# One base address and eight weight slabs: h starts at 480 modulo 512, and the gates of four output tiles are multiplied in the last SSD iteration

## The reference

```python
h = rmsnorm(x)
z, xBC, dt, q, f, i, g, gate_a, gate_b = split(h @ w_in)
y   = chunked_scan(conv(xBC), dt, state)          # Mamba-2 SSD, 8 groups
y   = grouped_rmsnorm((y + D * xs) * silu(z))     # 8 groups of 512 columns
y_a = y @ w_br_a                                  # 4096 -> 2048
y_b = hgrn2(q, f, i, g, state) @ w_br_b           # 2048 -> 2048
m   = sigmoid(gate_a) * y_a + sigmoid(gate_b) * y_b
x   = x + rmsnorm(m @ w_out)
x   = x + rmsnorm(relu(rmsnorm(x) @ w_up)**2 @ w_down)
x   = x + sigmoid(rmsnorm(x) @ w_ple_gate) * (p @ w_ple_proj)
```

## Time and profile before

| | us |
|---|---|
| median of 3 runs | 2816.43 |
| time of the profiled execution | 2817.92 |
| its span, first to last instruction | 2816.0 |
| TensorE busy | 2742.1 (97%) |
| VectorE busy | 1789.6 (64%) |
| ScalarE busy | 1425.6 (51%) |
| HBM read and written | 483.4 MB, 172 GB/s over the span |
| chain that ended last, by engine | PE 88%, DVE 7%, ACT 2%, issue 1%, DMA 1% |

### The profile page before, as it was taken

How to read it: one execution, slowest core, us unless ns; L and a number is a source line. 1 busy time by engine, 2 the same in 40 slices (tenths; PEclk the granted TensorE clock), 3 DMA queues, 4 the chain that set the end, 5 groups by cost and what they waited for, 6 DMA issues and landing times.

```text
span 2816.0 us, 59589 instructions
## 1 busy us (share of the span) xinstructions
PE 2742.1 (97%) x22075; PEld 2662.8 (95%) x22075; DVE 1789.6 (64%) x3208; ACT 1425.6 (51%) x2280; POOL 183.1 (7%) x297
## 2 busy tenths in 40 slices
PE   6999999999999999999979999989999999999999
PEld 5999999999999999999969999989999999999989
DVE  6878788744478887888854444566553345554475
ACT  5666666543356556556633333454443344443363
POOL 0111111100011111111110000000000000000000
PEclk9999999999999999999979999999999999999999
DMA  4544454455556665656535555535555545554534
GB/s 159 181 159 158 160 172 161 156 168 174 177 199 196 197 204 200 210 191 209 189 135 171 173 172 181 190 128 169 165 165 164 165 163 164 164 168 161 171 129 159
DMA packets 135286, 484.17 MB, mean 172 GB/s; under 512 B 17248, under 2 KB 19696, under 8 KB 134080
## 3 DMA queue, kind: packets, MB, share of 16 engines
q1 hardware_dynamic: 114560, 410.88, 43.8%
q0 software_dynamic: 20672, 72.55, 8.0%
HBM read 449.58 MB, written 33.78 MB: 172 GB/s over the span
## 4 chain that ended last, share of the span: by engine, by line
PE 88%; DVE 7%; ACT 2%; issue 1%; DMA 1%; POOL 0%; DVEq 0%; ACTq 0%; POOLq 0%
PE acc L1583 27%; PE acc L1585 26%; PE acc L1584 26%; DVE w_lo L967 1%; PE bank L1800 1%; PE bank L1846 1%; ACT w_hi L496 1%; PE bank L1749 1%; DVE ccv L1240 1%; PE bank L1830 1%; PE bank L1684 1%; PE bank L1766 0%; DVE x L1427 0%; DVE yf L1297 0%; DVE ht L1226 0%
## 5 line engine op out<-in xcount | busy, mean ns | idle before, releaser
L967 DVE TENSOR_TENSOR w_lo<-raw,w_hi 128x1024 fp32r<-128x1024 f32 x772 | 940.2, 1223 | 617.9 <-ACT w_hi L496 611.1
L1583 PE MATMUL acc<-h_hi,w_hi 128*128 128x288 f32 x3904 | 1169.6, 300 | 14.0 <-DVE h_lo L1003 11.5
L1584 PE MATMUL acc<-h_lo,w_hi 128*128 128x288 f32 x3904 | 1154.6, 296 | 0.0
L1585 PE MATMUL acc<-h_hi,w_lo 128*128 128x288 f32 x3904 | 1151.2, 295 | 0.0
L496 ACT ACTIVATE w_hi<-raw 128x1024 fp32r<-128x1024 f32 x772 | 811.3, 1055 | 463.8 <-PE acc L1585 408.0
L1583 PEld LDWEIGHTS acc<-h_hi,w_hi 128*128 128x128 f32 x3904 | 734.6, 188 | 21.7 <-issue 12.3
L1584 PEld LDWEIGHTS acc<-h_lo,w_hi 128*128 128x128 f32 x3904 | 735.9, 189 | 2.9
L1585 PEld LDWEIGHTS acc<-h_hi,w_lo 128*128 128x128 f32 x3904 | 737.7, 189 | 0.0
L1585 PE MATMUL acc<-u_hi,w_lo 128*128 128x288 f32 x1024 | 303.6, 296 | 0.0
L1583 PE MATMUL acc<-u_hi,w_hi 128*128 128x288 f32 x1024 | 302.6, 296 | 0.0
L1584 PE MATMUL acc<-u_lo,w_hi 128*128 128x288 f32 x1024 | 298.5, 292 | 0.0
(11 more groups left out here) (389 smaller groups left out, 3336.1 us busy)
## 6 DMA issues: line engine op xcount, KB each, us to landing
raw<-in_w SPq DMA_DIRECT2D x772, 512.0 KB, 3.3
ht<-in_ht POOLq DMA_DIRECT2D x64, 256.0 KB, 4.1
out_ssm_s<-ht POOLq DMA_DIRECT2D x64, 256.0 KB, 3.8
cbc<-cum_d POOLq DMA_DIRECT2D x8, 1152.0 KB, 6.9
hs<-in_s POOLq DMA_DIRECT2D x16, 512.0 KB, 4.5
out_hg_s<-hsn POOLq DMA_DIRECT2D x16, 512.0 KB, 5.0
x_in<-in_x SPq DMA_DIRECT2D x4, 576.0 KB, 6.0
mixb<-bmb POOLq DMA_DIRECT2D x16, 144.0 KB, 2.0
```

The costliest lines, as they stand in the source:

```text
L967: V.tensor_tensor(w_lo[:, k], raw[:, k], w_hi[:, k].bitcast(F32), ALU.subtract).then_inc(lo_done, 1)
L1583: M.matmul(out, w_hi[:, k, i], hi[:, kt0 + i], start=first and i == 0, stop=False)
L1584: M.matmul(out, w_hi[:, k, i], lo[:, kt0 + i], start=False, stop=False)
L1585: op = M.matmul(out, w_lo[:, k, i], hi[:, kt0 + i], start=False, stop=last and i == SK - 1)
```

## The change

First, `place[0] = aligned(place[0])` before h_hi and before the phase area: every base is rounded up to 480 modulo 512. Before, h_hi lies at byte 65664 and h_lo at 84096 of a partition (both 128 modulo 512); after, at 66016 and 84448 (both 480). The phase area, where o, y and u lie, moves from 111584 to 112096, which is 480 before and after; m stays at 192480 (480). The weights `w_hi` and `w_lo` stay at 32896 and 49280 (both 128). The constants move with h; `p_hi` comes to 480, `p_lo` stays at 224 modulo 512 at another address, and `p_in` takes the place of tok.

Second, the gate slabs of output tiles 0 to 3 (EARLY = 4) come first in the order of slabs: eight gate slabs, then 4 x 4 slabs of y. The eight are multiplied in the tail, into four banks; the y slabs of tiles 0 to 3 follow and use bank[2] and bank[3].

```diff
+EARLY = 4
 STORED = {}
+for _t in range(EARLY):
+    for _s in range(GA_SLABS):
+        STORED[U_GA + (2 * _t + _s if _s < 2 else 2 * EARLY + 4 * _t + _s - 2)] = U_GA + GA_SLABS * _t + _s
...
+    def aligned(at):
+
+        return (at - 480 + 511) // 512 * 512 + 480
...
+    place[0] = aligned(place[0])
     h_hi = sb("h_hi", [P, KT, T], F32R)
...
-    phase = place[0]
+    phase = place[0] = aligned(place[0])
...
+    gate_bank = (ps[0], ps[1], bank[0], bank[1])
...
+            def early_gate(u):
+
+                t = u // 2
+                if u % 2 == 0:
+                    if t < 2:
+                        free(T_GA + t, 0)
+                    elif t == 2:
+                        pe.wait_ge(sg_yf, 4 * GROUPS)
+                    else:
+                        pe.wait_ge(sg_spe, GROUPS)
+                multiply(*slab(U_GA, 2 * GA_SLABS, 0, u), gate_bank[t][:, 0:T], h_hi, h_lo, SK * (u % 2),
+                         u % 2 == 0, u % 2 == 1)
...
                 if not gemm:
+                    if s < 4:
+                        early_gate(s)
+                    if s in (7, 8):
+                        early_gate(s - 3)
+                    if s == 11:
+                        early_gate(6)
+                        early_gate(7)
                     continue
```

More of the change, by code:

```diff
@@ L697, in ssd @@
                 nxt(s)
+                if not gemm and s == 8:
+                    ahead(U_GA, 2 * GA_SLABS, 0, 3)
                 if not first and s == 8:
@@ L700, in ssd @@
                     nc.scalar.activation(yt, bank[5][:, :], ACT.Copy).then_inc(sg_yt, 1)
+                if not gemm and s == 9:
+                    ahead(U_GA, 2 * GA_SLABS, 0, 4)
                 if not first and s == 10:
@@ L703, in ssd @@
                     nc.scalar.activation(ysq, yf[:, :, :], ACT.Square).then_inc(sg_sq, 1)
+                if not gemm and s == 11:
+                    ahead(U_GA, 2 * GA_SLABS, 0, 5)
                 if not first and s == 12:
@@ L792, in branch_a @@
                 nc.scalar.activation(aya[:, :], ps[1][:, 0:T], ACT.Copy).then_inc(evac, 1)
[L793 to L798, removed]
+                merged_hi(t)
+        with act.Fori(EARLY // 2, KT // 2) as i:
+            branch_a(i)
         def out_tiles(i, first):
@@ L1289, in ssd @@
                         update({1: 0, 2: 2, 8: 4, 9: 6}[s])
+                    if not gemm and 1 <= s <= 4:
+                        ahead(U_GA, 2 * GA_SLABS, 0, s - 1)
+                    if not gemm and s in (11, 12):
+                        ahead(U_GA, 2 * GA_SLABS, 0, s - 7)
                     if s == 10:
@@ L1378, in _, with merge, branch_a @@
             if c in (1, 3):
-                ahead(U_GA, 2 * GA_SLABS, 0, c // 2)
-        def branch_a(i, first):
+                ahead(U_GA, 2 * GA_SLABS, 0, 6 + c // 2)
+        def merge(t):
+            dve.wait_ge(evac, t * 2 + (T_GA + 2))
+            dve.wait_ge(ga_in, t * 16 + 16)
+            V.scalar_tensor_tensor(aya[:, :], atg[:, :], 1.0, aya[:, :], ALU.add, ALU.mult).then_inc(ga_t, 1)
+            dve.wait_ge(ga_t, t + 1)
+            V.tensor_tensor(aya[:, :], aya[:, :], amb[:, :], ALU.add).then_inc(ga_m, 1)
+            dve.wait_ge(ga_hi, t + 1)
+            V.scalar_tensor_tensor(tile_at(m_lo, t), one(aya[:, :]), 0.5, tile_at(m_hi, t).bitcast(F32),
+                                   ALU.mult, ALU.subtract).then_inc(ga_lo, 1)
+        for t in range(EARLY):
+            for s in range(4):
+                ahead(U_GA, 2 * GA_SLABS, 0, 2 * EARLY + 4 * t + s)
+            merge(t)
+        def branch_a(i):
             for j in range(2):
-                t = i * 2 + j
-                for s in range(2 if first and j == 0 else 0, GA_SLABS):
+                for s in range(GA_SLABS):
                     ahead(U_GA, 2 * GA_SLABS, i, GA_SLABS * j + s)
[L1386 to L1397, removed]
+                merge(i * 2 + j)
+        with dve.Fori(EARLY // 2, KT // 2) as i:
+            branch_a(i)
         def weight(col, t):
@@ L1784, in ssd @@
                         new_states(2)
[L1785 to L1790, removed]
                     if s == 7:
@@ L1858, in _, with branch_a @@
         ssd(GROUPS, False, False)
-        def branch_a(i, first):
+        for t in range(EARLY):
+            if t < 2:
+                pe.wait_ge(sg_up, NB * GROUPS)
+            else:
+                pe.wait_ge(evac, T_GA + 2 * (t - 2) + 2)
+            for s in range(4):
+                multiply(*slab(U_GA, 2 * GA_SLABS, 0, 2 * EARLY + 4 * t + s), bank[2 + t % 2][:, 0:T], y_hi, y_lo,
+                         SK * s, s == 0, s == 3, (y_los, 0) if t == 0 else None)
+        def branch_a(i):
             for j in range(2):
-                for s in range(2 if first and j == 0 else 0, GA_SLABS):
+                for s in range(GA_SLABS):
                     if s in (0, 2):
@@ L1869, in branch_a @@
                     else:
[L1870 to L1875, removed]
+                        multiply(*at, ps[1][:, 0:T], y_hi, y_lo, SK * (s - 2), s == 2, s == 5)
+        with pe.Fori(EARLY // 2, KT // 2) as i:
+            branch_a(i)
         def out_tiles(i, first):
```

34 lines of the change are left out of this document (23 added, 11 removed).

## The result

| us | before | after |
|---|---|---|
| median | 2816.43 (2815.96 to 2818.28) | 2790.62 (2790.40 to 2791.71, 4 runs) |
| profiled execution, its span | 2817.92, 2816.0 | 2790.41, 2788.5 |
| h, second up stage, 512 first-pass matmuls | 204.4 | 202.7 |
| HGRN2, distance from one head to the next | 32.37 | 32.19 |
| SSD, distance from one group to the next | 81.08 | 80.89 |

The ratio is 0.9908 (95%: 0.9891 to 0.9925), the change is worth 25.8 us by the medians, 0.9%. 2788.0 was predicted with a range of 2781 to 2795. Old lines and new: 1583 to 1585 are now 1621 to 1623, 1749 is 1787, 1766 is 1804, 1758 is 1796, 1800 is 1845, 703 is 716, 967 is 995, 1376 is 1408, 2033 is 2092.

A forecast was written before the change was run, and what follows sets the result against it. TensorE was taken as the bound, busy 2742.1 of 2816.0 us. Terms of -13.2 (base address) and -15.2 (tail) sum to -28.4: 2789.5 profiled from 2817.92, 2788.0 as median, range 2781 to 2795.

The forecast's parts named there:

- Rival 2: The offset does nothing for h, which differs by lying just above the weights; 2801.2 us, chance 0.08.
- Rival 4: Slower than before: h's new offsets meet those of w_hi and w_lo in slow steps only; 2833.5 us, chance 0.04.
- the 0.2 I took off: Deduction in us from the 13.4 gained on h slabs, for places where TensorE arrives sooner only to wait.
- part 1: Base address: h takes u's rate, 3.173 for 3.200 us a slab, on 504 dense slabs; -13.2 us, bounds 0 to -14.5.
- Part 2: Tail: six gate slabs move into it, -19.2 us, less the delay to y; -15.2, bounds -21.5 to -10.7.
- (a): Tail, loads of ht: weight loads running beside them make ht arrive 4.0 us later; bounds 0 and 5.
- (b): Tail, gate slabs 0 to 3 on TensorE: they end at 1432.4, before ht lands, and delay nothing.
- (c): Tail, from ht's landing to the first y_lo: 0 us change, between -2.3 at full clock and +3.5 at half.
- (d): Tail, after the first y_lo: VectorE's list sets the pace, so tile 0 ends 17.1 us later, as before.
- (e): Behind tile 0, y slabs alone for tiles 1 to 3: splits and merge are covered by TensorE's 12.7 us.
- Rival 1: Tail: the loads don't collide and the clock holds, so Part 2 is -21.5; 2781.7 us, chance 0.20.
- rival 3: Tail: gate slabs wait for splits, the first y_lo slips 16 us, only 3.2 of Part 2 left; 2800.0, chance 0.06.

## Why the prediction was right, and where it was not

**The sign and the size of the offset, per matmul: right.** 202.7 in place of 204.4 is 132.2 ns a matmul in place of 133.3, as read from u, and the alternation of 0.78 and 0.81 came as said. Rival 2 (the offset does nothing) is out by the experiment with the offset alone. The Trainium skill, page "TensorE: Matmul & The Clock Gate", section "Back-to-back issue gap", gives N / 2.4 + 2.5 ns as the gap of an isolated matmul, and for streams of a weight load and a matmul about 81 ns at 128 columns and 131 at 512; the prediction left the second half out. The 132.2 and 133.3 ns measured at 288 columns are more than either gives, and neither has a term for addresses; the runs show two rates for one shape, sorted by addresses.

**The reason behind it: half right.** I took the rate as a property of the input's own offset. It is the distance to the weights that counts: with u and m untouched and only the weights moved, they lost what h had gained. Rival 4 had the right pair of tensors and the wrong sign: h lay in the slow relation already. The number came out because u and m had the distance +96 when I read them, and h got the same.

**How much of it reaches the end: wrong, the 0.2 I took off should have been 4 to 5.** Worked out from the two traces, part 1 gave 2.6 in the HGRN2 loop (first head to last, 480.85 to 478.21; 120 slabs, 3.2 by count), 1.2 in SSD iterations 1 to 7 (first ht matmul to the tail's old_states(0), 564.25 to 563.06; 140 slabs, 3.7 by count), 0.6 in gate_a, 1.4 in the first up stage, 1.7 in the second, 0.7 at the end: 8.2, where 13.4 - 0.2 were summed. The largest miss is the SSD loop: 0.19 a group in place of 0.53. From old_states(0), behind a group's first slab, to its sum of squares it is 42.16 us in both traces (1176.87 to 1219.03, and 1170.25 to 1212.41): that half is set by VectorE's and ScalarE's chain to xw, and TensorE's gain on the 11 slabs in it is handed back as a longer wait, 0.75 for 0.50. I had that very wait before me and charged it once, 0.2 in all, when it takes back this gain in each of the groups. A further 0.6 is missing in HGRN2, some 0.5 in the later stages, whose cause I didn't look for.

The 52 slabs of gate_b and of the SSD's first iteration, 1.4 by count, are in none of these terms, as their gain can't be told from noise: the stretch with them, from the last head to the first ht matmul, is 292.5 before and 289.5 after, but 289.5 too with h at its old place. Before's profiled execution had two more stretches at half clock there (3.4 us each), by chance. That is 3 us of the 27.5 by which the two profiled executions differ, and explains why they differ by more than the medians (25.8). So part 1 is 8.2 to 9.6 by the traces; the offset alone measured 8.9.

**Part 2: right, by its own terms.** -19.2 for six slabs stands. (a) ht was to be 4.0 later and is 3.0: the last load 14.4 after the first update (15.0 predicted, 12.1 before), the rest 3.9 (4.4 taken from the loop, 3.3 before). (b) the four slabs were done before ht came, with 4.70 left to wait. (c) was 0 between -2.3 and +3.5 and is +0.1: the clock was at half through the first half of slab 4, full for the rest, the middle case. That 0 was a choice between two bounds, not a sum, so its fit to 0.1 is luck. (d) 17.19 for 17.1. (e) nothing is visible: slabs 6 and 7 ended at their place, and first aya to first m is 19.75 shorter, which is 19.2 and the 0.6 of gate_a. The sum is -19.2 + 3.0 + 0.1 = -16.1; the two traces have 16.0 (338.3 to 321.8 from old_states(0) to the first m, less 0.6). -15.2 was predicted. The gates alone measured 14.3. In the loads of ht the collision was the right cause: without weight loads beside them landing is back at 16.70, and only there. Rival 1 (no collision, full clock) is thereby out, and rival 3 (a chain of slabs) too, as T slipped by 3.2 and not 16, and no gate slab in the tail waited for its split. The first y_lo came at 1447.95, inside the 1452 to 1458 less 6.7 of the prediction, but in part by luck: old_states(0) was 7.1 sooner, and 3 of that are the half-clock stretches in branch B.

**The number.** Part 1 was 3.6 to 5.0 too large and part 2 0.8 too small, which would make 2790.8 to 2792.2; measured is 2790.6. What remains, 0.2 to 1.6, is within the scatter of executions: the first HGRN2 head starts at 78.9 in the changed kernel's trace and at 81.1 in that of the offset alone, with the same work in front of it. So 2788.0 was 2.6 too low: most terms were right, the large miss, of part 1, was not, and the small one of part 2 paid back 0.8 of it.

## What to carry to other kernels

A gain per instruction counts only where that engine sets the pace: multiply it by the instructions in stretches without a wait behind them, and where a loop iteration has even a wait of 0.50, take the half in front of it as worth nothing until shown. When two dense streams of one shape run at different rates, move each operand by itself, the stationary one too, before believing in a property of the moving one. Filling a wait in part need not help: with half of the wait for ht filled the clock was at half for longer, during the work behind it, and T came no sooner; with the wait filled wholly the clock held until T and T came 1.5 sooner. Each of these is one trace, and neither moved the median.

## What the runs showed of the hardware

- Matmuls of 128x288 in fp32r, back to back, run at 133.3 or 132.2 ns by where the streamed tile lies past the weights modulo 128 bytes: +0 and +32 slow, +64 and +96 fast, in 21 readings of seven kernels (12 different pairs of offsets). With h_hi at +0 and h_lo at +96, or reversed, the rate is the fast one. Why, and whether other widths do the same, is open.
- Four loads of 512 KB on one queue beside four stores and four loads of 256 KB on another delay the last of these by 3.0 us (landing 16.45 to 16.70 in three traces without, 19.48 to 20.08 in the eight with the changed kernel's tail), and issuing the last store 0.4 sooner didn't help (20.79 in one trace).
- In the wait of 4.70 for ht the clock fell, and was at half for 6.8 us; 0.4 behind the end of one of 2.36 (five gate slabs before it) it fell for 10.2; in that of 4.39, with sparse work behind it, for 27.3. With no wait (six slabs before it) the clock was full until 1450.3. Besides, stretches of 3.4 at half clock come and go between executions in which the code is the same: before the tail there are three in the trace of the kernel before, and one in that of the gates alone. They are not to be read as an effect of an edit.
